# A gated DeltaNet encoder step in fp32: state-chain steps spread one place later over the levels, one projection piece moved ahead of the block product

## What is computed

```python
proj = h @ w_in                                     # q, k, v, z for each head
q, k, v = silu(causal_dwconv4(proj[qkv]))           # q and k then l2-normed
# per head and chunk:
A  = strict_lower(beta_i * (k k^T) * gamma)
Tm = inverse(eye + A)                               # triangular
u, w = Tm @ (v * beta), Tm @ (k * beta * exp(decay))
def step(S, xs):
    v_new = u_c - w_c @ S
    o = qd_c @ S + attn_c @ v_new
    S = S * dl_c + kt_c^T @ v_new
    return S, o
y = (rmsnorm(o) * g_norm * silu(z)) @ w_out
```

## Time and profile before

| | us |
|---|---|
| median of 3 runs | 3392.69 |
| lowest, highest of them | 3390.32, 3394.24 |
| the profiled execution | 3392.9 |
| its span in the trace | 3391.2 |
| PE busy (share of the span) | 3115.3 (92%) |
| mean granted TensorE clock, share of full | 0.965 |

### The profile page before, as it was taken

How to read it: one execution, slowest core, us unless ns; L and a number is a source line. 1 busy time by engine, 2 the same in 40 slices (tenths; PEclk the granted TensorE clock), 3 DMA queues, 4 the chain that set the end, 5 groups by cost and what they waited for, 6 DMA issues and landing times. The chain is left out here.

```text
span 3391.2 us, 54197 instructions
## 1 busy us (share of the span) xinstructions
PE 3115.3 (92%) x19666; PEld 2993.4 (88%) x19666; DVE 1526.8 (45%) x3265; ACT 838.0 (25%) x1761; POOL 1152.3 (34%) x991
## 2 busy tenths in 40 slices
PE   5988998899876999999999799999679999999998
PEld 5888888888766999999999689999679999999997
DVE  4567666666643433333433433433334333334334
ACT  2333343334422210011101224444312101110112
POOL 3333232323115443444343141312055334443430
PEclk8999999999978999999999899999789999999999
DMA  3000100010003111111111110101031111111101
GB/s 130 26 22 13 27 21 21 12 27 21 2 3 114 50 44 43 45 48 49 43 37 37 51 45 21 39 21 32 2 114 51 50 37 53 45 43 43 49 25 51
DMA packets 206909, 136.67 MB, mean 40 GB/s; under 512 B 32120, under 2 KB 198832, under 8 KB 206576
## 3 DMA queue, kind: packets, MB, share of 16 engines
q1 hardware_dynamic: 206832, 135.63, 13.5%
HBM read 120.98 MB, written 14.63 MB: 40 GB/s over the span
## 5 line engine op out<-in xcount | busy, mean ns | idle before, releaser
L91 PE MATMUL ps<-act_hi,ffn_hi 128*128 128x352 f32 x2496 | 811.7, 325 | 61.4 <-POOL ffn_lo L147 59.9
L93 PE MATMUL ps<-act_hi,ffn_lo 128*128 128x352 f32 x2496 | 804.8, 322 | 0.0
L92 PE MATMUL ps<-act_lo,ffn_hi 128*128 128x352 f32 x2496 | 804.0, 322 | 0.0
L145 POOL TENSOR_TENSOR ffn_hi<-ffn_stage,one 128x512 fp32r<-128x512 f32 x296 | 320.4, 1082 | 1033.9 <-PE ps L93 899.0
L91 PEld LDWEIGHTS ps<-act_hi,ffn_hi 128*128 128x128 f32 x2496 | 471.0, 189 | 67.0 <-issue 53.8
L92 PEld LDWEIGHTS ps<-act_lo,ffn_hi 128*128 128x128 f32 x2496 | 472.2, 189 | 0.8 <-issue 0.2
L93 PEld LDWEIGHTS ps<-act_hi,ffn_lo 128*128 128x128 f32 x2496 | 471.3, 189 | 0.0
L147 POOL TENSOR_TENSOR ffn_lo<-ffn_stage,ffn_hi 128x512 fp32r<-128x512 f32 x296 | 407.0, 1375 | 23.2
L750 DVE TENSOR_TENSOR x<-x,ps 128x352 f32<-128x352 f32 x528 | 273.2, 521 | 212.9 <-PE ps L93 212.9
L92 PE MATMUL ps<-ffn_hid_lo,ffn_hi 128*128 128x352 f32 x1056 | 341.4, 323 | 0.0
L93 PE MATMUL ps<-ffn_hid_hi,ffn_lo 128*128 128x352 f32 x1056 | 340.8, 323 | 0.0
(11 more groups left out here) (314 smaller groups left out, 5161.4 us busy)
## 6 DMA issues: line engine op xcount, KB each, us to landing
ffn_stage<-in_ffn_w_gu SPq DMA_DIRECT2D x88, 512.0 KB, 3.7
ffn_stage<-in_ffn_w_down SPq DMA_DIRECT2D x44, 512.0 KB, 3.5
gdn_stage<-in_gdn_w_in SPq DMA_DIRECT2D x32, 512.0 KB, 4.1
x_kept<-x SPq DMA_DIRECT2D x2, 4224.0 KB, 12.8
x<-x_kept SPq DMA_DIRECT2D x6, 1408.0 KB, 7.8
ml_stage<-in_ml_w_in SPq DMA_DIRECT2D x16, 512.0 KB, 4.2
load_rows<-in_x_prompt SPq DMA_DIRECT2D x8, 512.0 KB, 4.4
ffn_stage<-in_gdn_w_out SPq DMA_DIRECT2D x8, 512.0 KB, 4.0
```

The source lines that it names most:

```text
L91: pe.matmul(out, w_hi, rhs_hi, start=first, stop=False)
L92: pe.matmul(out, w_hi, rhs_lo, start=False, stop=False)
L93: return pe.matmul(out, w_lo, rhs_hi, start=False, stop=last)
L145: nc.gpsimd.tensor_tensor(hi, st, one, ALU.mult).then_inc(self.hi_done, 1)
```

## The change

The pieces at level 0 are divided 4 and 1 in place of 3 and 2, so that one more stands ahead of step 0 and of the block product. A new table `steps` says which chain step stands at which place. For batches 1 and 2 steps 0 to 2 stay; step 3 moves from level 1 B to level 2 A, and each of steps 4 to 8 one place further, so that step 8 stands at level 4 B. The fourth round is as before. On VectorE `join` of level 2 (L1432) now stands ahead of the level's first step. The same `chain_at` replaces the two tests in TensorE's, ScalarE's and VectorE's `head`; the left-out part of the diff is ScalarE's.

```diff
@@ -775,7 +775,16 @@
-        return {"P": (8, 5, 5)[r], "A": (3, 3, 2, 1, 1, 1, 1)[l], "B": (2, 2, 1, 1, 1, 1, 1)[l]}[place]
+        return {"P": (8, 5, 5)[r], "A": (4, 3, 2, 1, 1, 1, 1)[l], "B": (1, 2, 1, 1, 1, 1, 1)[l]}[place]
+
+
+    def steps(r, l, place):
+
+        if r == 0:
+            return ()
+        if r == BATCHES:
+            return tuple(s for s in (2 * l + "AB".index(place),) if s < 9)
+        return {0: (0, 1), 1: (2, None), 2: (3, 4), 3: (5, 6), 4: (7, 8)}.get(l, (None, None))["AB".index(place):][:1]
@@ -1076,6 +1085,11 @@
+            def chain_at(t, r, l, place):
+                for s in steps(r, l, place):
+                    if s is not None:
+                        chain_step(t, r - 1, s)
@@ -1095,14 +1109,12 @@
                         pieces(r, l, "A")
-                        if r > 0 and 2 * l < 9:
-                            chain_step(t, r - 1, 2 * l)
+                        chain_at(t, r, l, "A")
                         if r < BATCHES:
                             join_z(t, r, l, pieces)
                         else:
                             pieces(r, l, "B")
-                        if r > 0 and 2 * l + 1 < 9:
-                            chain_step(t, r - 1, 2 * l + 1)
+                        chain_at(t, r, l, "B")
...
@@ -1469,21 +1484,24 @@
                     for l in range(LEVELS):
-                        if r < BATCHES and l < 2:
+                        if r < BATCHES and l < SOLVED:
                             join(t, r, l)
-                        if r > 0 and 2 * l < 9:
-                            chain_step(t, r - 1, 2 * l)
-                        if r < BATCHES and l >= 2:
+                        chain_at(t, r, l, "A")
+                        if r < BATCHES and l >= SOLVED:
                             join(t, r, l)
                         for u in O_FINISH[l] if r == 0 and past else ():
                             finish(t - 1, u)
-                        if r > 0 and 2 * l + 1 < 9:
-                            chain_step(t, r - 1, 2 * l + 1)
+                        chain_at(t, r, l, "B")
```

## The result

The changed kernel takes 3371.65 us (median of 4 runs, 3369.31 to 3374.18) against 3393.11 us before (4 runs, 3390.32 to 3394.24): a ratio of 0.9935, with 95% of 0.9919 to 0.9950, or 21.5 us less. Its profiled execution has a span of 3372.0 us (3391.2 before) at the same granted clock of 0.965.

A forecast was written before the change was run, and what follows sets the result against it. PE, busy 92% of the span, was taken as the bound, its idle time and clock as winnable. 7 x (0.48 - 1.4 - 0.8) = -12.0, head 7 -1.5, clock -3: 3392.9 - 16.5 = 3376 us, range 3363 to 3386.

The forecast's parts named there:

- T: The start of step 3 on PE; said to be set by block product L1026 and VectorE, and to stay.
- The piece ahead of the block product: Level 0, one more piece before L1026: free in batches 1 and 2, +0.48 us in batch 0 of seven heads.
- Batch 1, -1.4: Batch 1 of seven heads: step 3 one place later, two pieces ahead of T, step 7's wait gone: -1.4 us each.
- two pieces less behind T: Level 2 A, batch 1: two pieces now run in PE's idle time ahead of T, 0.96 us less behind it.
- Batch 2, -0.8: Batch 2 of seven heads: the same step move, less waits for ScalarE's silus: -0.8 us each, between -1.2 and 0.
- the second silu: Batch 2, ScalarE: next head's silu (1.09 us) now ahead of level 5's wz copy, with step 8's output copy: +0.4 us.
- Head 7, -1.5: The head without pieces: transposes no longer wait for step 3's y; -1.5 us in all, between -4 and +1.
- the table load: Head 7, batch 2, ScalarE: a table load of 1.28 us falls ahead of level 5's copy, +0.9 us.
- The clock, -3: PE's clock falls from 2.4 to 1.2 GHz for a part after step 3: six falls for eight, -3 us.
- A: Rival: with shorter waits all or nearly all clock falls vanish, another 8 to 10 us, 3366 us; chance 0.18.
- B: Rival: the wait only moves, VectorE or ScalarE setting the pace of levels 3 to 5; 3387 us, chance 0.20.
- C: Rival: VectorE's two level 2 taps delay step 5's state update, so step 6 waits; slower, 3407 us, chance 0.05.

The follow-up runs named there:

- e9_before_pool: The kernel before with GpSimd's splits of two weight quarters moved to levels where VectorE has slack: 3347.32 us, ratio 0.9867.
- e10_pieces: The kernel before with only the two pieces of level 2 A moved to level 1 B in batches 1 and 2, steps unmoved: 3387.54 us, ratio 0.9984.
- e3_join: The changed kernel with VectorE's old order at level 2, the solved blocks (L1432) behind step 3's y: 3391.04 us, ratio 0.9995 to the kernel before.
- e7_silu: The changed kernel with the second silu of batch 2 moved from level 4 to level 5: 3364.82 us, ratio 0.9919 to the kernel before.
- e2_fill: The kernel before with only the piece moved ahead of the block product (4 and 1 at level 0): 3395.49 us, ratio 1.0014.
- e1_steps: The changed kernel without the piece moved ahead of the block product (3 and 2 at level 0): 3361.46 us, ratio 0.9914 to the kernel before.
- e5_more: The changed kernel with batch 0's old fill, four pieces fewer in its prepare, two more at level 2 A of batches 1 and 2: 3354.24 us.
- e6_pool: e1_steps with GpSimd's splits of two weight quarters moved to levels where VectorE has slack: 3323.17 us, ratio 0.9796 to the kernel before.
- e8_both: e6_pool with the second silu of batch 2 moved from level 4 to level 5: 3322.88 us, ratio 0.9792 to the kernel before.
- e11_after_pool: The changed kernel with GpSimd's splits moved as in e6_pool: 3328.58 us, ratio 0.9811 to the kernel before.

## Why the prediction was right, and where it was not

The forecast was 3376 us, 16.5 less than the profiled execution; measured were 3371.65, inside the range, 21.5 less between the medians and 19.2 between the profiled spans. By its steps:

- **T is set by the block product and VectorE**: right. 7.52 to 7.49 us in batch 1, 7.17 to 7.18 in batch 2; the waits at step 3 are 2.15 and 1.81, as said. e9_before_pool shows it from the other side.
- **The piece ahead of the block product**: right. Free in batches 1 and 2, +0.49 in batch 0 (+0.48 said). The transposes wait 1.15 us there (1.2 said, 0.71 in the earlier trace rows):

```profile
371.09 0.54 PE L1042 MATMUL ps<-ident,gdn_z 128*128 128x128 f32 x3 [1.15 <-DVE gdn_z L1447]
```

- **Batch 1, -1.4**: measured -1.6 like for like. T to transposes went from 1.51 to 0.54 (0.6 said), from there to level 5 from 9.79 to 9.14; T to level 5 is 9.68 where the clock stays (9.9 said). But the reason was told incompletely. I counted "two pieces less behind T" as 0.96 us by itself; e10_pieces does just that and wins nothing in this batch, and e3_join, with the pieces moved but L1432 behind y, loses the 0.95 again. The term is worth its price only because VectorE writes z ahead of y. The sum was right as both parts were in the change.
- **Batch 2, -0.8**: the largest error in size, measured -1.5. T to level 5 is 10.10 us (10.2 said), and the wait for the second silu is there (0.55 us at 444.63, 0.4 said). But level 5 to 6 was to grow by 0.3 and shrank from 4.06 to 3.81. I let the old wait of 0.57 us at level 6 absorb only a part, as if its length came from PE's work alone. It came from the row of VectorE ahead of it: the small copies L1328 took 1.08 us and the tap L1351 1.86 beside a split. GpSimd's splits, which follow the level 4 product, now end at T + 12.7 us in place of T + 14.2, while the copies start at T + 10.7 in place of T + 11.5, so less of them stands beside a split. VectorE in batch 2, first the kernel before (head 1), then the changed one (head 2):

```profile
334.55 0.38 DVE L1328 TENSOR_SCALAR gdn_raw<-gdn_hist 128x3 f32 x1
334.85 1.08 DVE L1328 TENSOR_SCALAR gdn_tails<-gdn_raw 128x3 f32 x2
```

```profile
443.35 0.63 DVE L1343 TENSOR_SCALAR gdn_raw<-gdn_hist 128x3 f32 x1
443.90 0.23 DVE L1343 TENSOR_SCALAR gdn_tails<-gdn_raw 128x3 f32 x2
444.16 1.72 DVE L1366 TENSOR_SCALAR gdn_qkv<-gdn_raw,gdn_head_conv_w 128x1059 f32<-128x1059 f32 x1
```

  The shortening is read from the traces; no run isolates it.
- **Head 7, -1.5**: measured 99.64 to 99.25 us from its first `prepare` on, -0.4. The two terms came as said. T to level 5 of batch 2 went from 10.82 to 9.66 (-1.2 said), and the table load lengthened the wait behind it from 0.57 us to 1.48, +0.9. The kernel before, the changed kernel's ScalarE, and its PE:

```profile
1000.55 0.94 PE L1044 MATMUL ps<-gdn_wz,gdn_z 128*128 128x128 f32 x6 [0.57 <-ACT gdn_wz L1230]
```

```profile
980.83 1.28 ACT L1300 ACT_TABLE_LOAD   x1
982.12 0.48 ACT L1242 COPY gdn_wz<-ps 128x384 f32<-128x384 f32 x1
```
```profile
982.66 0.94 PE L1053 MATMUL ps<-gdn_wz,gdn_z 128*128 128x128 f32 x6 [1.48 <-ACT gdn_wz L1242]
```

  Batch 1 even gained 1.7. What took it back had no term in the sum: 0.24 us in batch 0, 0.46 between the block product and T of batch 2, and 0.9 behind level 6, where the clock fell at an earlier product. These are not the change's doing as far as the runs show: in e7_silu, whose program is the same in head 7, that head is 4 us shorter. So -0.4 is one reading of a number that moves by more.
- **The clock, -3**: wrong. Two falls fewer were forecast; there are eight before and eight after in these batches, moved from batch 2 (five to one) into batch 1 (three to seven). A fall costs 1.2 us in the new batch 1 and 1.5 before, which with one fall fewer brings 3.2 us in heads 1 to 5. Heads 0 and 6 take the same back, 1.6 of it by the fall in batch 0 of head 0. The sum is about 0.
- **The rivals.** A (the clock stays up) did not come about, though the time lies close to its part of the range: there are as many falls as before. B (the wait only moves): in heads 0 to 6 no product of levels 3 to 5 waits 0.5 us but L1053 of level 5 in batch 2. By the letter that 0.55 us was a sign of B; it is the silu's wait, which the sum had priced, and the batch gained all the same. C (the state of step 5 behind the taps): that state is ready at 406.60, 1.2 us ahead of step 6's L1074 at 407.77; the cushion was put at 1.3. Nor was it the taps that it came behind: they end at 404.73, and VectorE then idles for PE's increment of the state. And the tap ahead of the level 3 mask took 0.77 us, not 1.35: the sentence on the Trainium skill had said that the taps of batch 1 would gain by its rule, and this row agrees.

So -12.0 for the seven heads was -18.3, -1.5 for head 7 was -0.4, and -3 for the clock was about 0. Ahead of head 0 (+1.6) and behind DeltaNet (-2.2) the two programs do the same work, and the traces differ by that much. Between the spans the forecast was short by 2.7 us: batch 2 (7 x 0.7) and batch 1 (7 x 0.2) brought 6.3 more than said and the stretches outside 0.6 more, the clock and head 7 brought 4.1 less. The remaining 2.3 us up to the 21.5 of the medians are scatter between executions. The mechanism was right; that the sum came so near is in part luck, as errors of both signs cancelled. Two rivals were added up loosely: B's terms make -6.5 us, 3386 and not 3387, and C takes batch 2's gain at 1.1 us where the sum has 0.8. Neither touches the forecast.

## What to carry to other kernels

Ask first what sets the time for which an engine waits: work put ahead of the wait is free only if that start does not move, and here it was a gain only once the engine that is waited for no longer had a second result queued behind the first which the next product also needs. So the order on the engine that is waited for changes with the order of the one that waits, or the gain stays as a new wait. And a wait that ends on a row of small operations is looked at from the side of that row's neighbours: here another engine's work, moved by a few levels, was worth more than twice what the change won.

## What the runs showed of the hardware

- **VectorE beside GpSimd.** The 21 operations of at most 7 elements took 3.64 us alone and 5.9 beside L928, L145 and L147 (5.6 in batch 2); the longest single one took 1183 ns where the median was 218. The tap L1351 of 1059 elements took 0.77 us alone, 1.35 beside a mask and 1.72 to 1.86 beside splits. Moving two quarters' splits won 46 us of 3393 in the kernel before, as TensorE waits for those 21 operations in 14 batches.
- **The clock does not follow the wait's length alone.** In batches 1 and 2 of heads 0 to 6 every fall began between 0.3 us ahead of step 3 and 2.9 us behind it. In batch 2 the clock fell after a wait of 2.3 us in five of seven heads before, after 1.8 in one of seven in the changed kernel, and after 2.75 in all seven of e2_fill. But in batch 1 of e2_fill it stayed up after 3.1 us in six of six. After 1.3 us it fell in none of seven batches 2 of e1_steps and in six of seven of e10_pieces. In the five kernels in which the wait at step 3 was 1.25 us or less (e5_more, e6_pool, e8_both, e9_before_pool, e11_after_pool) it fell in none of 70 batches. A fall cost 0.7 to 1.7 us, those of twice the length in e3_join 2.2 to 2.4. What else decides it stays open; the way to be rid of it was to be rid of the wait.
- **The same program does not take the same time everywhere.** Head 7 took 99.3 us in the changed kernel and some 4 less in e7_silu with the same instructions, and the stretch behind DeltaNet 2364 to 2372 us over the twelve profiled executions. A difference of a few us there says nothing about a change made elsewhere; the batch lengths of heads 1 to 5 with the clock alike, equal to 0.1 us, do.
